# Gate and up products of the experts in native float32 on four groups of 32 columns, with their weights unsplit in a ring

## The reference

```python
def swiglu(h, wg, wu, wd):
    return (jax.nn.silu(h @ wg) * (h @ wu)) @ wd

def moe_swiglu(h, w_router, wg, wu, wd):
    logits = (h @ w_router).astype(jnp.float32)
    top_v, top_i = lax.top_k(logits, TOP_K)
    gate = jax.nn.softmax(top_v, axis=-1)
    comb = jnp.sum(jax.nn.one_hot(top_i, N_EXPERTS, dtype=jnp.float32) * gate[..., None], axis=-2)
    out = jnp.zeros_like(h)
    for e in range(N_EXPERTS):
        out = out + comb[..., e:e + 1] * swiglu(h, wg[e], wu[e], wd[e])
    return out
```

## Time and profile before

| | us |
|---|---|
| three runs | 1620.6, 1619.97, 1615.33 |
| median | 1619.97 |
| profiled execution | 1616.93 |
| its span | 1614.0 |
| TensorE matmuls busy | 1589.2 |
| VectorE busy | 1265.8 |
| ScalarE busy | 1017.2 |
| first product of the experts' stage | at 646.43 |
| last turn of the loop | at 1594.54 |

### The profile page before, as it was taken

The page is one execution under the profiler, slowest core; times in us unless marked ns, Lnnn a source line. Parts: engine busy times, 40 slices in busy tenths (PEclk is TensorE's granted clock), DMA queues, the critical chain, the costliest instruction groups (busy, mean ns, idle before and its releaser), DMA issues.

```text
span 1614.0 us, 20610 instructions
## 1 busy us (share of the span) xinstructions
PE 1589.2 (98%) x8097; PEld 1325.3 (82%) x8097; DVE 1265.8 (78%) x1136; ACT 1017.2 (63%) x985; POOL 73.3 (5%) x63
## 2 busy tenths in 40 slices
PE   8999999999999999999999999999999999999997
PEld 7778888888887888888888888888888888888886
DVE  5757566666776656998899899889889889889895
ACT  6643443434564434677777777777777777777774
POOL 1000000000000001000000000010010010010010
PEclk9999999999999999999999999999999999999999
DMA  8524335555552545799999999999999999999993
GB/s 331 210 105 157 131 124 200 184 206 198 183 190 84 203 160 211 292 399 388 382 389 374 369 391 376 378 380 372 380 385 375 377 387 367 372 376 365 387 398 129
DMA packets 39613, 470.65 MB, mean 292 GB/s; under 512 B 4480, under 2 KB 4752, under 8 KB 10000
## 3 DMA queue, kind: packets, MB, share of 16 engines
q1 hardware_dynamic: 35280, 454.33, 72.7%
q0 software_dynamic: 3856, 14.49, 2.9%
q10 hardware_dynamic: 432, 1.19, 0.2%
HBM read 463.18 MB, written 6.82 MB: 291 GB/s over the span
## 4 chain that ended last, share of the span: by engine, by line
PE 78%; DMA 11%; DVE 5%; issue 3%; ACT 3%; POOL 0%; SPq 0%; POOLq 0%; DVEq 0%; ACTq 0%
PE PS L844 19%; PE PS L846 19%; PE PS L845 19%; DMA stage<-wm_dram 9%; PE PS L1134 9%; PE PS L1135 4%; DVE wlo L1968 3%; ACT whi L723 2%; PE PS L1363 1%; DMA w1v<-wl_dram 1%; PE PS L1196 1%; PE PS L1176 1%; PE PS L916 1%; DVE wlo L1475 1%; PE PS L935 1%
## 5 line engine op out<-in xcount | busy, mean ns | idle before, releaser
L1968 DVE TENSOR_TENSOR wlo<-stage,whi 128x2048 fp32r<-128x2048 f32 x330 | 740.5, 2287 | 99.6 <-ACT whi L723 99.3
L723 ACT ACTIVATE whi<-stage 128x2048 fp32r<-128x2048 f32 x328 | 610.7, 1912 | 207.4 <-DMA stage<-wm_dram 198.4
L844 PE MATMUL PS<-whi,e_hi 128*128 128x512 f32 x896 | 355.5, 397 | 0.0
L846 PE MATMUL PS<-whi,e_lo 128*128 128x512 f32 x896 | 349.9, 390 | 0.0
L845 PE MATMUL PS<-wlo,e_hi 128*128 128x512 f32 x896 | 348.9, 389 | 0.0
L1475 DVE TENSOR_TENSOR wlo<-stage,whi 128x2048 fp32r<-128x2048 f32 (+2 forms) x58 | 185.3, 3194 | 93.7 <-ACT whi L444 93.6
L444 ACT ACTIVATE whi<-stage 128x2048 fp32r<-128x2048 f32 (+2 forms) x61 | 162.9, 2675 | 96.1 <-PE PS L846 52.3
L846 PEld LDWEIGHTS PS<-whi,e_lo 128*128 128x128 f32 x896 | 168.2, 188 | 36.1
L845 PEld LDWEIGHTS PS<-wlo,e_hi 128*128 128x128 f32 x896 | 168.6, 188 | 33.2
L844 PEld LDWEIGHTS PS<-whi,e_hi 128*128 128x128 f32 x896 | 168.4, 188 | 33.1 <-issue 0.3
L844 PE MATMUL PS<-whi,a_hi 128*128 128x512 f32 x448 | 175.5, 392 | 0.8 <-DVE a_lo L2056 0.7
(11 more groups left out here) (345 smaller groups left out, 1804.4 us busy)
## 6 DMA issues: line engine op xcount, KB each, us to landing
stage<-wm_dram SPq DMA_DIRECT2D x168, 2048.0 KB, 9.8
stage<-wl_dram SPq DMA_DIRECT2D x20, 2048.0 KB, 7.8
stage<-wf_dram SPq DMA_DIRECT2D x33, 1024.0 KB, 4.7
stage<-wl_dram SPq DMA_DIRECT2D x4, 1816.0 KB, 8.8
w1k<-wl_dram SPq DMA_DIRECT2D x2, 2048.0 KB, 8.4
w1v<-wl_dram SPq DMA_DIRECT2D x2, 2048.0 KB, 8.1
third<-wl_dram SPq DMA_DIRECT2D x2, 1816.0 KB, 9.8
xs<-mem_dram POOLq DMA_DIRECT2D x2, 1024.0 KB, 8.2
```

The source lines that it names most:

```text
L723: nc.scalar.activation(whi[kind][:, half], stage[kind][:, half], ACT.Copy).then_inc(w_hi[kind] if part else half_hi[kind], 1)
L844: mm(out, ah, bh, start=start, stop=False)
L846: return mm(out, al, bh, start=False, stop=stop)
L1968: ins = V.tensor_tensor(wlo[kind][:, half], stage[kind][:, half], f32(whi[kind][:, half]), ALU.subtract)
```

## The change

CAP becomes 96. The gate and up weights are no longer split. They are loaded into a ring of seven tiles of 2 MB, which takes the places of two sets of stage, hi and lo buffers and some others; only the down weights still pass through `stage[2]`, `whi[2]` and `wlo[2]`. The gathered tokens are kept as one float32 tile `e_in`. For each k the 96 slots are three pieces of 32 stationary columns on column groups 0 to 2, with 384 moving columns each, and the fourth group takes the other 128 columns for each of the three pieces in turn:

```diff
-CAP = 128
+CAP = 96
+PIECE = 32
+RING = 7
...
+            def up_e(it, s, kind, first):
+                p, n = 2 * s + kind, it * MOE_STEPS + s
+                r, turn_ = p % RING, p // RING
...
+                if not (first and s == 0):
+                    pe.wait_ge(f_mul if kind else f_silu, n + FF_STEPS)
+                w = ring[r]
+                for k in range(KD):
+                    if kind == 0 and s == 0 and k % 4 == 0:
+                        pe.wait_ge(e_ready, it * 2 + (k // 4 + 1))
+                    for t in range(3):
+                        rows = slice(t * PIECE, (t + 1) * PIECE)
+                        mm(bank(kind)[rows, 0:3 * P], e_in[:, k, rows], w[:, k, 0:3 * P], start=(k == 0), stop=(k == KD - 1),
+                           skip_group_check=True)
+                    for t in range(3):
+                        ins = mm(bank(kind)[CAP:P, t * P:(t + 1) * P], e_in[:, k, t * PIECE:(t + 1) * PIECE], w[:, k, 3 * P:4 * P],
+                                 start=(k == 0 and t == 0), stop=(k == KD - 1), skip_group_check=True)
+                ins.then_inc(w_used[kind], 1)
```

Silu and multiply then work on 128 partitions x 384 columns, with no scale, and three transposes turn them. The turned values fall into two parts, which `turned_hi` and `turned_lo` bring into the order of the down weights' rows; the down product has 96 stationary columns. The turn of step n moves behind the down product of step n-1:

```diff
                     for kind in range(2):
...
-                            ins = product(bank(kind), e_hi[:, k, :], e_lo[:, k, :], wh[:, k, :], wl[:, k, :], k == 0, k == KD - 1)
-                        ins.then_inc(w_used[slot], 1)
-                        if kind == 0 and not begin:
-                            turn(n)
+                        up_e(it, s, kind, first)
                     if s == MOE_STEPS - 1:
                         turn_rows(it + 1)
                     if not begin:
                         if s == 1 and not first:
                             pe.wait_ge(md_hi, it)
                         down_e(n, s == 1, s == 0)
+                    turn(n)
```

The normalisation moves from silu and multiply to the rows: `gather_hi` scales by the reciprocal root mean square and so waits for it, and `gather_lo(0)` moves behind it, in front of the router's chain. `x_rows` is written from `x_normed`, which ScalarE makes after `e_in` of the first item:

```diff
             def gather_hi(t):
-                act.wait_ge(x_half, 4 + 2 * t + 2)
-                nc.scalar.activation(xs_hi[:, t, :], x[:, t, :], ACT.Copy).then_inc(fn_hi, 1)
+                act.wait_ge(f_rstd, NT + t + 1)
+                nc.scalar.activation(xs_hi[:, t, :], x[:, t, :], ACT.Copy, scale=stat[:, 6 + t:7 + t]).then_inc(fn_hi, 1)
...
-            pool.dma_start(x_rows.rearrange("(t p) d -> p t d", p=P), x[:]).then_inc(put_done, 16)
             pool.dma_start(sums[0:SEQ, :].rearrange("(t p) d -> p t d", p=P), x[:]).then_inc(put_done, 16)
+            pool.wait_ge(fn_hi, 2 * NT + 2 * NT)
+            pool.dma_start(x_rows.rearrange("(t p) d -> p t d", p=P), x_normed[:]).then_inc(put_done, 16)
```

SyncE issues the load of a ring tile when TensorE has used what lay in it seven tiles before, and the load of a down tile when VectorE has split the last one:

```diff
+                for p in range(RING if first else 0, 2 * MOE_STEPS):
+                    kind = (p - RING) % 2
+                    sp.wait_ge(w_used[kind], it * MOE_STEPS + ((p - RING) // 2 + 1 + MOE_USED[kind]))
+                    load_up(e, p)
+                    s = (p - RING) // 2
+                    if p % 2 and not (first and s == 0):
+                        sp.wait_ge(w_lo[2], it * MOE_STEPS + (s + MOE_FILLS[2]))
+                        load_down(e if s >= 0 else e_before, s % MOE_STEPS, 2)
```

More of the change, by code:

```diff
@@ L747, in _ @@
             half_square(1, 1, 1)
-            gather_hi(1)
-            def down_parts():
-                nc.scalar.activation(down_hi[:].rearrange("p (b n) -> p b n", b=2), PS[:, 2:4, :], ACT.Copy, scale=gate_slot).then_inc(md_hi, 1)
+            for t in range(NT):
+                gather_hi(t)
             def rows_of(it):
@@ L772, in item @@
                     begin = first and s == 0
-                    if not begin and not (first and s == 1):
-                        mhi(0, n)
                     if s == 0:
@@ L782, in item @@
                     if begin:
-                        mhi(0, 1, True)
+                        act.wait_ge(pos_done, 2)
+                        for t in range(NT):
+                            normed(t)
                         act.wait_ge(rv, RV_DIF)
                         nc.scalar.activation(rt[:, 260:262], rt[:, 258:260], ACT.Exp).then_inc(r_exp, 1)
-                    if first and s == 1:
-                        mhi(1, 1)
-                        mhi_half(2, 0, 0)
-                    elif not begin:
-                        mhi(1, n)
@@ L801, in item @@
-                    if s == 0:
-                        act.wait_ge(slot_ready, it + 1)
-                    nc.scalar.activation(hid_tok[:, 0, :], bank(0), ACT.Silu, scale=rstd_slot).then_inc(f_silu, 1)
-                    if not begin:
-                        act.wait_ge(mt_done, n + 0)
-                        nc.scalar.activation(a_hi[:], bank(4), ACT.Copy).then_inc(ma_hi, 1)
-                    if first and s == 1:
-                        mhi_half(2, 0, 1)
-            act.wait_ge(cross_out, 4 * DEPTH)
@@ L811, in _ @@
-            mhi(1, 0, True)
+                    else:
+                        turned_hi(n)
+                        if s == 1 and not first:
+                            act.wait_ge(w_used[2], it * MOE_STEPS + MOE_USED[2])
+                            rows_of(it)
+                        for part in range(2):
+                            down_hi_half(n - 1, part)
+                    act.wait_ge(w_used[0], n + (MOE_USED[0] + 1))
+                    if not begin:
+                        act.wait_ge(f_mul, n + FF_STEPS)
@@ L1359, in turn, with turned, down_product @@
             def turn(n):
[L1361 to L1362 removed]
+                pe.wait_ge(f_mul, n + (FF_STEPS + 1))
+                for c in range(3):
                     ins = nc.tensor.transpose(bank(4)[:, c * P:(c + 1) * P], hid_tok[:, 1, c * P:(c + 1) * P], ident)
                 ins.then_inc(mt_done, 1)
+            def turned(a, c):
+                return a[:, c * CAP:(c + 1) * CAP]
+            def down_product(hf, c, wh, wl, start, stop):
+                out = bank(2 + hf)[0:CAP, :]
+                ah, al = turned(a_hi, c), turned(a_lo, c)
+                return product(out, ah, al, wh, wl, start, stop)
             def down_e(n, start, stop):
[L1368 removed]
+                pe.wait_ge(half_lo, n)
                 pe.wait_ge(ma_lo, n)
@@ L1429, in _ @@
             steps = n_items * MOE_STEPS
-            pe.wait_ge(f_mul, steps + FF_STEPS)
-            for c in range(4):
-                ins = nc.tensor.transpose(bank(4 + c // 2 * 2)[:, c % 2 * P:(c % 2 + 1) * P], hid_tok[:, 1, c * P:(c + 1) * P], ident)
-                if c % 2:
-                    ins.then_inc(mt_done, 1)
             pe.wait_ge(oh_ready, n_items + 2)
```

289 lines of the change are left out of this document (124 added, 165 removed).

## The result

The changed kernel takes 1633.65 us in the median (four runs, 1631.42 to 1641.1) against 1618.68 us (the three runs above and a fourth), a ratio of 1.0099 with a 95% interval of 1.0079 to 1.012: **slower by 1.0%, 15 us**. I had forecast 5 us faster, within a range whose upper end was 1642. In the profiled execution the span grows from 1614.0 to 1633.2 us, by 19.2.

A forecast was written before the change was run, and what follows sets the result against it. TensorE was taken as the bound (98% of the span, 16.8 us a step), with DMA a close second limit. -7 + 1.2 + 1.2 + 0.6 - 1 = -5 us, so 1619.97 - 5 = 1615 us, range 1604 to 1642.

The forecast's parts named there:

- One step: Experts' stage, gate and up plus group visit plus one turn fewer: -0.13 us a step, -7 us over 55 steps.
- A: Gate and up: groups don't pack when passes are unequal, 0.5 us a step, 27 us in all: 1642; chance 0.2.
- Gate and up: Float32 products on four column groups: fourth group sets the pace, 0.654 us per k, 10.46 us, 0.42 less a step.
- the visit to the groups: Going into column groups and out again, once a step on TensorE: costs 0.40 us.
- Rival B: Gate and up: filling and emptying come with every k, 0.76 us per k, 95 us in all: 1710; chance 0.05.
- Splits of gate and up: Splits on VectorE and ScalarE go, beside TensorE: nothing gained; remaining down weights have some 2.5 us of slack.
- Head and first step: Before the experts' first product, a subtraction moved forward: +1.2 us; first step, multiply not hidden by down: +1.2 us.
- Tail: Last turn to last down: split now in series, about 2.0 us instead of 1.40, +0.6 us.
- Waits: TensorE's 2.4 us of waits for loads should shrink with the weight ring: -1 us.
- Rival C: DMA holds the beat at 380 GB/s, the item stays at 119 us: +3 us, 1623; chance 0.12.
- the sum of -5 us: Whole kernel: steps -7, head +1.2, first step +1.2, tail +0.6, waits -1.

The follow-up runs named there:

- hinted version: The changed kernel with its loop kept and a prefetch hint for the closing branch at the top of every iteration: 1611.26 us, 0.9951 to the kernel before.
- halved kernel: The changed kernel with loop and no hint, gate and up products taking only four of eight input blocks: 1606.89 us in one run.
- split one: The hinted version with the first down tile's high part taken before step 0's silu, its low part right behind the multiply: 1610.27 us, 0.9939.

## Why the prediction was wrong

**The step that failed** is "One step: -0.42 + 0.40 - 0.11 = -0.13 us, over 55 steps -7 us". It multiplies a step by 55 and has no term for what stands between items: the loop's return, 0.2 us and covered in the kernel before, cost 16.5 us in six gaps and 6.8 us of clock after four. The step itself was right. No rival had the return either: the 1642 us of A came from a mechanism that the runs don't show, and that my range holds the result through it is luck. A number that could have warned me was in my own text: each float32 matmul "leaves two records". I used it for the time of a pass and not for the length of the loop's body, which grows from 1,130 to 3,133 instructions; that 3,133 are too many, only the runs show.

The rest can be read from the hinted version, which has the same work. Its first and last branch are at 879.1 and 1586.8, in the kernel before at 875.4 and 1590.6, in the changed kernel at 878.9 and 1610.1:

| | to the first branch | six items | from there to the end | span |
|---|---|---|---|---|
| before | 875.4 | 715.2 | 23.4 | 1614.0 |
| changed | +3.5 | +16.0 | -0.3 | +19.2 |
| hinted | +3.7 | -7.5 | -0.6 | -4.4 |

- **Steps: right, somewhat better.** By the chain of the hinted version, a step between two turns is 16.67 us (1253.49 to 1270.16), as forecast for one of them, and six items gain 7.5 us where 42 x 0.13 gave 5.5. The item before is 119.2 us on average over the loop, not 119.0.

```profile
1253.16 0.33 PE PS L1370 x3
1253.49 0.25 PE PS L1410
...
1269.83 0.33 PE PS L1370 x3
1270.16 0.25 PE PS L1410
```

- **Gate and up** (0.654 us per k, 10.46) and **the visit to the groups** (0.40): right together within 0.05 us a step (16.67 against 16.76 - 0.13 = 16.63); no run shows the 0.40 us of the visit by itself, only the step that has it in its sum. Rival B's 0.76 us per k would have made the block 12.2 us; it took 10.62.
- **Splits of gate and up** gain nothing: right. Their engines' free time shows only as less busy time on the page.
- **Head and first step**: to the first product of the stage +2.5 us in the changed kernel (648.96 against 646.43), not +1.2, and +4.2 in the hinted one (650.58), where the clock was at 0.50 from 638.63 to 645.46; the changed one ran there at full clock. So +1.3 us of the head have no term in my sum. The first steps lost another 1.9 us in the changed kernel: from the start of step 2's gate and up to its down product took 11.71 instead of 10.62 us, and the down block 6.44 instead of 5.64. Both are waits for the low part of the second down tile (1.02 and 0.57 us), for which I had seen some 2.5 us of slack. The hinted one lost only the second.
- **Tail**: 1.79 us from the last turn to the last down against a forecast of 2.0.
- **Waits**: the gain of 1 us didn't come. 1.8 us of waits for the down weights, nearly all in the first steps, and 0.6 for a_lo replace the 2.4.
- **Rival C** had more truth than its 0.12: the down tile's circle takes 16.5 us in the halved kernel, only 0.2 us less than a step of the changed one. I had given it 9.8 + 6.5 = 16.3 us without setting that against the step. At a step of 16.51 us (the run without most of the fourth group's passes) TensorE still waited for it only 0.6 us between 700 and 1500, with the loads at 385 GB/s and a share of 0.97. How far the loads alone could go is not shown.

All in all the sum of -5 us stands for the hinted version (-4.4 in the profile, -7 in the medians, by the interval -10 to -6). It is, with the split one, the fastest complete kernel here: 0.5% under the kernel before, 1.4% under the changed one.

## What to carry to other kernels

When a change multiplies instructions (native float32, smaller column groups, more pieces), count the loop's body per engine (here 1,130 instructions became 3,133) and look at the row of its closing branch before adding up steps. Here a branch of 0.21 us and no instruction packets in later rounds went with the bodies of up to 1,662, and a branch of 4.8 to 6.8 us with a stall at every return of the bodies from 1,774 on; a hint at the loop's top or straight code took the 16.5 us of gaps away without touching the work. Idle time for "issue" at regular distances was a place in the code here, not a missing buffer.

## What was not expected of the hardware

- A loop body of 1,662 instructions came back in 0.21 us and one of 1,774 in 6.3. In the four kernels whose body is that long or longer and has no hint, the branch back took 4.8 to 6.8 us, and the queued matmuls ran on for some 4 us of it. Most of this is not the transfer: in the six returns of the changed kernel the packet of 16 KB starts 3.5 to 4.1 us after the branch, takes 0.9 to 1.0 us, and the branch ends 1.4 to 1.5 us after it has landed. What fills the time before and behind it is not shown.
- With the hint the same branch takes 0.7 us in the median, 2.15 us at most.
- TensorE's granted clock fell to 0.50 for 3.4 us after single idle times as short as 1.82 us (6.8 us after the one of 4.67), and it stayed at 1.00 after others as long as 3.05 us.
- Native float32 passes of 384 columns on three groups and of 128 on the fourth run side by side, each group at its own pace: 0.645 us per k for the three, 0.654 for the fourth.
